# Final norm and first sliding layer's norm joined behind the projection, and squares added in pairs for the mLSTM output norm

## The reference, cut to what matters

```python
def rmsnorm(x, g):
    y = xf * lax.rsqrt(jnp.mean(xf * xf, axis=-1, keepdims=True) + EPS)
    return (y * g.astype(jnp.float32)).astype(x.dtype)

# first_block ends:   x = x + squared_relu_mlp(rmsnorm(x, ff_ln[l]), ff_w1[l], ff_w2[l])
#                     return rmsnorm(x, final_ln)
# second_block:       h = concatenate([meta, x]); for each layer: u = rmsnorm_2(h, norm_gain[i]); h = h + mixer(u)
# mlstm_branch ends:
    h = rmsnorm_2(h, h_gain.reshape(B_HEADS, B_DV)).reshape(bsz, lp, B_W)
    return (h * jax.nn.silu(z.astype(jnp.float32))).astype(u.dtype) @ w_out
```

## Time and profile before

| | before |
|---|---|
| time, median of 3 runs | 3629.98 us (3616.33 to 3632.56) |
| the profiled execution: time | 3631.66 us |
| the profiled execution: span from first to last instruction | 3629.8 us |
| mean granted TensorE clock | 0.976 |
| busy: TensorE matmul | 3461.8 us (95%) |
| busy: TensorE weight load (overlaps the matmuls) | 2727.9 us (75%) |
| busy: VectorE | 1997.6 us (55%) |
| busy: ScalarE | 716.1 us (20%) |
| busy: GpSimd | 84.5 us (2%) |
| moved by DMA | 251.98 MB, mean 69 GB/s |

### The profile page before, as it was taken

How to read it: one execution, slowest core, us unless ns; L and a number is a source line. 1 busy time by engine, 2 the same in 40 slices (tenths; PEclk the granted TensorE clock), 3 DMA queues, 4 the chain that set the end, 5 groups by cost and what they waited for, 6 DMA issues and landing times.

```text
span 3629.8 us, 43978 instructions
## 1 busy us (share of the span) xinstructions
PE 3461.8 (95%) x16715; PEld 2727.9 (75%) x16715; DVE 1997.6 (55%) x4671; ACT 716.1 (20%) x1763; POOL 84.5 (2%) x100
## 2 busy tenths in 40 slices
PE   8987999999999999999999898999999999999988
PEld 3365688888854558888888765888887888887766
DVE  4353167554413783675544658644354656557566
ACT  2221011110012560111100125012212111121143
POOL 0000000000000000000000011000000000000110
PEclk9988999999999999999999999999999999999999
DMA  3100322222211003212222130222211222102311
GB/s 129 49 21 12 111 74 70 82 93 82 105 58 47 13 19 112 80 70 82 93 82 93 59 94 14 92 70 76 73 65 45 95 80 86 43 24 83 110 43 47
DMA packets 39367, 251.98 MB, mean 69 GB/s; under 512 B 5708, under 2 KB 5836, under 8 KB 11008
## 3 DMA queue, kind: packets, MB, share of 16 engines
q1 hardware_dynamic: 31616, 224.41, 17.5%
q10 hardware_dynamic: 4496, 11.89, 1.2%
q0 software_dynamic: 3056, 12.96, 1.1%
HBM read 240.58 MB, written 2.16 MB: 67 GB/s over the span
## 4 chain that ended last, share of the span: by engine, by line
PE 88%; DVE 8%; issue 2%; ACT 1%; DMA 1%; ACTq 0%; POOL 0%; POOLq 0%; DVEq 0%
PE PL L1213 26%; PE PX L1213 20%; PE PL L921 14%; PE PL L1561 4%; PE PL L1408 3%; PE PL L905 2%; PE PX L1670 2%; DVE SCR L2971 2%; PE PL L1326 1%; DVE SCR L2986 1%; PE PL L1586 1%; PE PX L1346 1%; PE PL L1713 1%; PE PX L931 1%; PE PL L1375 1%
## 5 line engine op out<-in xcount | busy, mean ns | idle before, releaser
L921 PE MATMUL PL<-xn,ring 128*128 128x264 f32 (+1 forms) x1600 | 506.6, 474 | 10.8 <-DVE xn L2365 10.2
L921 PEld LDWEIGHTS PL<-xn,ring 128*128 128x128 f32 x1600 | 305.8, 193 | 198.1 <-issue 165.4
L2408 DVE TENSOR_TENSOR Z<-PL,SCR 128x512 f32<-128x512 f32 (+3 forms) x104 | 63.8, 614 | 469.8 <-PE PL L921 372.0
L1213 PE MATMUL PL<-Z,ring 128*128 128x256 f32 (+1 forms) x1248 | 297.3, 388 | 10.5 <-DVE Z L3361 8.6
L1213 PEld LDWEIGHTS PL<-Z,ring 128*128 128x128 f32 x1248 | 240.7, 193 | 49.9 <-DVE Z L3361 10.1
L1213 PE MATMUL PL<-AUX,ring 128*128 128x256 f32 (+1 forms) x1056 | 243.9, 379 | 0.0
L1213 PEld LDWEIGHTS PL<-AUX,ring 128*128 128x128 f32 x1056 | 200.6, 190 | 27.6 <-DVE AUX L2739 0.2
L1213 PE MATMUL PL<-xn,ring 128*128 128x264 f32 (+1 forms) x864 | 204.1, 388 | 12.7 <-DVE xn L2365 11.5
L1213 PEld LDWEIGHTS PL<-xn,ring 128*128 128x128 f32 x864 | 165.7, 192 | 43.1 <-issue 12.4
L1841 ACT ACTIVATE SCR<-PL 128x256 f32<-128x256 f32 (+1 forms) x72 | 27.7, 384 | 737.1 <-PE PL L1213 737.1
L1213 PE MATMUL PX<-Z,AUX 128*128 128x264 f32 (+1 forms) x704 | 163.8, 384 | 2.7 <-DVE Z L3169 2.7
(11 more groups left out here) (515 smaller groups left out, 6055.2 us busy)
## 6 DMA issues: line engine op xcount, KB each, us to landing
ring<-w_tiles SPq DMA_DIRECT2D x212, 1024.0 KB, 4.8
Z<-Z ACTq DMA_DIRECT2D x16, 264.0 KB, 5.1
SCR<-head_rows POOLq DMA_DIRECT2D x16, 264.0 KB, 3.7
AUX<-norm_scratch POOLq DMA_DIRECT2D x8, 528.0 KB, 6.6
cst<-consts ACTq DMA_DIRECT2D x1, 2188.5 KB, 14.9
resid<-x ACTq DMA_DIRECT2D x4, 512.0 KB, 8.8
AUX<-mem POOLq DMA_DIRECT2D x2, 1024.0 KB, 5.1
AUX<-w_cmp POOLq DMA_DIRECT2D x1, 2048.0 KB, 10.6
```

Of the source, the lines that this page charges most:

```text
L921: mm = pe.matmul(PL[:, 2 * h + c, 0:e - a], ring[t % 2][:, k, P * h:P * h + P], src_block(name, k)[:, a:e], start=k == 0, stop=k == KB - 1)
L1213: mm = pe.matmul(ps, lhs(k), rhs(k), start=kc == 0 and k == 0, stop=kc == per - 1 and k == 3)
L2408: ins = dve.tensor_tensor(d, ps, f, ALU.mult)
```

## The change

**The two norms are joined.** With r the final norm's factor of a token, f its gain and g the gain of A0's norm, the input of A0_in is x f g times one factor per token, since r cancels but for epsilon: the factor is 1 / sqrt(mean(x^2 f^2) + eps (mean(x^2) + eps)). `prepare("final", b)` now writes x f g into `X2` inside f21 as each block is finished. Beside the plain sum of squares, VectorE keeps one weighted by f^2 (`joint_squares`, into `joint_acc`), and joins the two after the head sums. `joint_tables`, ahead of the work of f21's tile 9, makes the products of the gains and does the 16 meta columns. TensorE's ones-sum of the joint squares stands behind m7 of A0_in's first tile, its ones-sum of the final norm ahead of the second tile's m1. The final norm is applied to the residual stream in A0_in: its reciprocal after tile 1, its products after tiles 2 and 3, four blocks each. A0 comes ahead of the final norm in the table of norms, and A0's products use PSUM banks as A1's do. POOL's load of a small table for A0 still waits for the final norm to be applied.

**Squares in pairs.** Ahead of the copies of the first three units, VectorE adds the mLSTM's squares two by two in place, and TensorE sums 8 pairs and not 16 blocks: 3, 3 and 2 behind the three units.

```diff
--- before
+++ after
-CONSTS = [("ones", 128), ("eps", 2), ("ident", 128), ("half_swap", 128),
+CONSTS = [("ones", 128), ("eps", 3), ("ident", 128), ("half_swap", 128),
...
+_norm("A0", 0, 1)
 _norm("final", 8, 1)
-_norm("A0", 8, 1)
...
-            if name[:2] == "A0":
-                at = 2
-            elif at is None:
+            if at is None:
...
+        joint_gain, final_squared = tiny[:, 216:224], tiny[:, 224:232]
+        joint_acc = AUX[:, 9792:9792 + T2]
+        meta_sq = AUX[:, 9792 + T2:9792 + T2 + 8 * META].rearrange("p (b t) -> p b t", b=8)
...
+                if name == "A0":
+                    pe.wait_ge(joint_done, 1)
+                    for c, a, e in halves(T):
+                        mm = pe.matmul(PX[:, at + c, 0:e - a], K("ones"), joint_acc[:, a:e], start=True, stop=True)
+                    mm.then_inc(joint_sum, 1)
+                    return
+                if name == "final":
+                    at = 1
+                    pe.wait_ge(norm_std, rooted("A0"))
...
+            def pair_row_sum(p):
+
+                N = NORM["B_h"]
+                at = 2 * (N["index"] % 2)
+                pe.wait_ge(pair_sum, p + 1)
+                for c, a, e in halves(T2):
+                    mm = pe.matmul(PX[0:8, at + c, 0:e - a], K("sum_row", 7 - p, 15 - p),
+                                   sq_buf[:, (N["block0"] + 2 * p) % 4, a:e], start=p == 0, stop=p == 7)
+                mm.then_inc(norm_sq_used, 2)
...
-                                if prepared and prepared[:2] != "xa":
+                                if prepared and prepared[:2] != "xa" and prepared != "A0":
                                     norm(prepared)
                             pe.wait_ge(qd_s, QUAD_TILE0[name] + t + 1)
+                        if name == "A0_in" and (t, i) == (0, 4):
+                            norm("A0")
+                        if name == "A0_in" and (t, i) == (1, 0):
+                            norm("final")
...
-                        for b in range(6 * i, min(6 * i + 6, 16)):
-                            row_sums("B_h", b)
+                        for p in range(3 * i, min(3 * i + 3, 8)):
+                            pair_row_sum(p)
...
-                    act.wait_ge(*((final_block, b + 1) if b < 7 else (norm_done, normed("final"))))
...
-                act.wait_ge(norm_sq_used, N["block0"] + N["per"] * N["groups"])
+                if name == "A0":
+                    act.wait_ge(joint_sum, 1)
+                else:
+                    act.wait_ge(norm_sq_used, N["block0"] + N["per"] * N["groups"])
                 act.wait_ge(norm_done, N["before"]) if N["before"] else None
-                rows = P if N["groups"] == 1 else N["groups"]
-                act.activation(pair(std_buf[0:rows, N["index"] % 2, 0:T], T), psb(PX[0:rows], 2 * (N["index"] % 2), T),
-                               ACT.Sqrt, scale=inv, bias=K("eps", 0, 1)[0:rows]).then_inc(norm_std, 1)
+                rows, eps = P if N["groups"] == 1 else N["groups"], 2 if name == "A0" else 0
+                at = 1 if name == "final" else 2 * (N["index"] % 2)
+                act.activation(pair(std_buf[0:rows, N["index"] % 2, 0:T], T), psb(PX[0:rows], at, T),
+                               ACT.Sqrt, scale=inv, bias=K("eps", eps, eps + 1)[0:rows]).then_inc(norm_std, 1)
...
+                    if i == 0 and g == 1:
+                        norm_root("final")
...
-                if name != "final":
-                    ins = dve.tensor_scalar(dst[b], src[b], gain[b], None, ALU.mult)
+                if name == "final":
+                    ins = dve.tensor_scalar(X2[:, b, META:T2], src[b], joint_gain[:, b:b + 1], None, ALU.mult)
                     ins.then_inc(*((norm_done, 1) if b == 7 else (xn_block, 1)))
+                    if 2 <= b < 7:
+                        joint_squares(b - 1)
+                        add_squares(name, b - 1)
+                    return
+                ins = dve.tensor_scalar(dst[b], src[b], gain[b], None, ALU.mult)
+                ins.then_inc(*((norm_done, 1) if b == 7 else (xn_block, 1)))
                 if b >= 2:
                     add_squares(name, b - 1)
                 if b == 7:
                     add_squares(name, 7)
+
+            def joint_squares(b):
+
+                first, tokens = NORM["final"]["block0"], joint_acc[:, META:T2]
+                if b == 1:
+                    dve.wait_ge(norm_sq, first + 1)
+                    counted(dve.tensor_scalar(tokens, acc_buf[:, 0:T1], final_squared[:, 0:1], None, ALU.mult))
+                dve.wait_ge(norm_sq, first + b + 1)
+                dve.wait_ge(dve_step, own[0])
+                counted(dve.scalar_tensor_tensor(tokens, sq_buf[:, (first + b) % 4, 0:T1], final_squared[:, b:b + 1], tokens,
+                                                 ALU.mult, ALU.add))
+
+            def joint_tables():
+
+                final, first = Q("final_ln"), Q("norm_gain", 0, 8)
+                counted(dve.tensor_tensor(joint_gain, final, first, ALU.mult))
+                counted(dve.tensor_tensor(final_squared, final, final, ALU.mult))
+                meta = resid[:, :, 0:META]
+                for b in range(8):
+                    dve.tensor_scalar(X2[:, b, 0:META], meta[:, b, :], first[:, b:b + 1], None, ALU.mult)
+                step(dve.tensor_tensor(meta_sq, meta, meta, ALU.mult))
+                step(dve.tensor_tensor(meta_sq[:, 0:4], meta_sq[:, 0:4], meta_sq[:, 4:8], ALU.add))
+                step(dve.tensor_tensor(meta_sq[:, 0:2], meta_sq[:, 0:2], meta_sq[:, 2:4], ALU.add))
+                counted(dve.scalar_tensor_tensor(joint_acc[:, 0:META], meta_sq[:, 0, :], D * (EPS - EPS * EPS) / P,
+                                                 meta_sq[:, 1, :], ALU.add, ALU.add))
...
-                        if name == "final" and b:
-                            ins.then_inc(final_block, 1)
...
+                    if name == "f21" and t == 9:
+                        joint_tables()
...
-                    for b in range(8):
-                        dve.wait_ge(*((final_block, b + 1) if b < 7 else (norm_done, normed("final"))))
-                        prepare(n, b)
                     dve.wait_ge(norm_done, normed(n))
                     sums_head(n + "_in", 0, (0, 4))
+                    for b in (6, 7):
+                        joint_squares(b)
+                        add_squares("final", b)
+                    dve.wait_ge(norm_sq_used, NORM["final"]["block0"] + 7)
+                    dve.wait_ge(dve_step, own[0])
+                    tokens = joint_acc[:, META:T2]
+                    dve.scalar_tensor_tensor(tokens, acc_buf[:, 0:T1], EPS, tokens, ALU.mult, ALU.add).then_inc(joint_done, 1)
                     sums_tail(n + "_in", 0, (0, 4))
 
                 def tables(t):
+
+                    if i == 0 and t == 1:
+                        norm("final")
+                    if i == 0 and t in (2, 3):
+                        x, _, gain, _, T = norm_spec("final")
+                        for b in range(4 * t - 8, 4 * t - 4):
+                            ins = dve.scalar_tensor_tensor(x[b], x[b], gain[b], factors("final"), ALU.mult, ALU.mult)
+                        if t == 3:
+                            ins.then_inc(norm_done, 1)
...
+                    for p in range(3 * i, min(3 * i + 3, 8)) if i < 3 else ():
+                        one, two_ = (sq_buf[:, (N["block0"] + 2 * p + j) % 4, :] for j in range(2))
+                        dve.wait_ge(norm_sq, N["block0"] + 2 * p + 2)
+                        dve.tensor_tensor(one, one, two_, ALU.add).then_inc(pair_sum, 1)
...
-    c["eps"] = np.broadcast_to(np.array([EPS, 1.0])[None, :], (P, 2))
+    c["eps"] = np.broadcast_to(np.array([EPS, 1.0, EPS * EPS])[None, :], (P, 3))
```

More of the change, by code:

```diff
@@ L251, in build @@
         out_sem = sem("out_sem")
-        final_block = sem("final_block")
+        pair_sum = sem("pair_sum")
+        joint_done, joint_sum = sem("joint_done"), sem("joint_sum")
         dn_kk, dn_d, dn_exp, dn_at = (sem(n) for n in ("dn_kk", "dn_d", "dn_exp", "dn_at"))
@@ L462, in build @@
         assert 2 * (NORM["xa1"]["index"] % 2) == 0 and 2 * (NORM["ff1"]["index"] % 2) == 2
-        assert [2 * (NORM[n]["index"] % 2) for n in ("A0", "B", "C", "A1")] == [2, 0, 0, 0]
+        assert [2 * (NORM[n]["index"] % 2) for n in ("A0", "B", "C", "A1")] == [0, 0, 0, 0]
         xk, xv = blocks(Z, MEM, 16, 8), blocks(Z, MEM, 24, 8)
@@ L1750, in _ @@
                     nsa()
-                elif layer == "final":
-                    norm("final")
                 elif layer in ("win0", "win1"):
@@ L1756, in _ @@
                     mlstm()
-                else:
+                elif layer == "hgrn":
                     hgrn()
@@ L1793, in prepared_square @@
                         act.wait_ge(x_in[0], 16)
-                    elif host is None:
-                        act.wait_ge(psum_free, evacuated("f21"))
                     else:
@@ L2324, in _ @@
```

(4 more changed lines are left out.)

5 lines of the change are left out of this document (2 added, 3 removed).

## The result

| | this kernel | before | ratio | 95% interval |
|---|---|---|---|---|
| median of 11 runs each, us | 3610.98 (3603.65 to 3612.53) | 3628.36 (3616.33 to 3632.56) | 0.9948 | 0.9941 to 0.9956 |
| profiled execution, us (span; granted clock) | 3603.65 (3601.9; 0.980) | 3631.66 (3629.8; 0.976) | | |

The ratio makes it 18.9 us or 0.52% faster (0.44 to 0.59% by the interval). That is just beyond the 0.5% which the prediction took for the least that can be told from no change, and the interval reaches to both sides of it. The forecast was 3608. The two profiled executions lie 28.0 us apart and not 18.9, since that of after is the shortest of its runs.

A forecast was written before the change was run, and what follows sets the result against it. TensorE was taken to bound the kernel (busy 95% of the span, 88% of the chain). Savings of 17.6 + 4.6 = 22.2 us take the profiled 3631.66 to 3609.5; with the median 1.7 lower, forecast 3608, range 3598 to 3622.

The forecast's parts named there:

- Part one: From f21's last matmul to tile 1 of A0_in: joining the norms saves 17.6 us.
- the wait at m6: In A0_in's first tile, TensorE waits 1.3 us at product m6 for VectorE's two head sums.
- the tail sum that m5 needs: In A0_in's first tile, VectorE's tail sum is ready within 0.2 us of when m5 needs it.
- The split of it: Of the saving before A0_in's tile 1, some 12.5 us is idle time and 5.1 the half clock.
- The moved work: VectorE's work moved into f21 and A0_in is covered by its idle time and costs nothing.
- Rival C: VectorE's moved work in A0_in is not hidden and costs 8.7 us: 13.5 gained, 3616 us; chance 0.08.
- Part two: Row sums in B_z: pairs save 4.6 us, 7.3 without waits, with two new TensorE waits of 1.3 us.
- Rival B: In B_z ScalarE's squares pace the sums, so pairs save towards nothing: 17.6 us alone, 3612; chance 0.10.
- D: No wait at m6 of A0_in and none in B_z's row sums: 26.2 us gained, 3604; chance 0.07.
- Rival A: Three short TensorE pauses of about 1.3 us also lower the clock, 5.1 us per fall: 3613 to 3618; chance 0.12.
- Rival E: Slower: the clock stays low in A0_in after the pause is gone; all at half gives +53 us, 3683; chance 0.03.
- The sum, 22.2: Whole kernel: 17.6 us before A0_in's tile 1 plus 4.6 us in B_z make 22.2 us saved.

The follow-up runs named there:

- experiment 9: The kernel before with eighteen needless matmuls behind the final norm's ones-sum, so that TensorE keeps working; one execution, 3626.23 us.
- experiment 7: The changed kernel with the final norm's reciprocal and all eight products in one piece after tile 1 of A0_in; one execution, 3602.87 us.
- also alone: The kernel before with only the mLSTM's squares summed in pairs, without the joined norms; ratio 0.9991 to the kernel before.
- experiment 8: The changed kernel with the joint ones-sum behind m2 of A0_in's first tile and not behind m7; one execution, 3617.16 us.
- the three comparisons: The changed kernel, unedited, run three times against the kernel before; ratios 0.9948, 0.9943 and 0.9944.

## Why the prediction was right, and where its steps were off

The forecast of 3608 with "faster" as the likeliest held: 3610.98. Point by point:

**Part one, minus 17.6.** Measured minus 17.97; tile 1 stands at 15.28 or 15.29 in all seven traces that have this order. The order of events was as worked: block 7 in time for the eighth matmul, m6 waiting for the head sums, the joint sum free of waiting, tile 1 at 15.28 and not 15.7. The term mis-sized is the wait at m6: the step was "TensorE waits 1.3 us", and it is 1.00 from start to start (0.84 as a gap). VectorE came through sooner than durations set one after another gave, because rows overlap by their tails: from the scaling of block 6 to the end of that of block 7 it took 2.72 us, and I had 2.9. Another 0.2 was put down for the tail sum that m5 needs; TensorE had no wait there (m5, m3 and m4 take 5.34 us from 1996.27 to 2001.61).

**The split of it was wrong.** "Some 12.5 of this is idle time and 5.1 the half clock" takes m1 and m2 from 7.9 us busy to 3.6 as if TensorE alone paced them. The row of the second head sum shows that VectorE would have held m6 back anyway, and in experiment 9 four of m1's records at full clock gained nothing. By the rows the half clock had on the path the final ones-sum (0.85) and at most 0.45 at m6; the rest of the 18 us is VectorE's chain. The sum was right since I compared both ends of the stretch, not because I knew what lay in between.

**The moved work.** Costed at nothing, and nothing is what it cost: TensorE has no wait behind any of it. joint_tables took 2.16 us where I took 2.5, and TensorE waits nowhere in the tiles around it. But the reason given, "each piece is shorter than the 4.24 us that VectorE idles between a tile's end and the next m2", is not the limit (and the idle time ends with m6, not m2): experiment 7 put 8.7 us into one piece and TensorE did not wait. So "nothing" was right for a reason that was wrong. Rival C falls.

**Part two, minus 4.6.** Measured minus 4.56, also alone. The waits were put at 1.3 and are 1.12 each, and 4.05 us for a group of three pairs, which I had at 4.0. Rival B falls, since ScalarE's pace does not reach the other six pairs, and D falls, since the waits are there.

**Rival A** falls for this change: the clock is 1.00 behind the pauses of 0.84 and 1.12 us. The Trainium skill ("TensorE: Matmul & The Clock Gate", section "A second HAM failure mode: psum-queue depth-cycling") tells of a kernel in which TensorE idles briefly between groups of matmuls so often that the clock swings between its two levels. These pauses, one or two at a time between long work, showed none of that. The one of 4.09 us in experiment 8 and the 2.30 us of the earlier trace rows did go with a fall. Nor can the rival be set aside by the length of a pause, as the prediction did with "no row here shows a fall behind a pause of 1.3 us": in experiment 9 the clock fell in a wait of 1.33 us, shortly behind one of 1.00. **Rival E** falls: A0_in had 1.00 throughout. The half clock of the earlier trace rows lies in a run of 32 records of one column each (from 1050.41 to 1055.73), and A0_in has nothing like it.

**The sum, 22.2.** The touched stretches give 22.5, the three comparisons 18.9, 20.7 and 20.3. Of the 1.8 to 3.6 us between them 0.8 has a place, which the prediction did not name: "to B_z" is 0.7 to 0.9 us longer in seven of the eight traces with the joined norms (1.5 in that of experiment 8). There the clock falls sooner. TensorE, behind a wait for ScalarE's small copy, takes 2.12 us for four short records, and 1.33 in the kernel before: after the change the clock is down during the wait (0.53 from 2092 to 2093), and before it falls only as these records end (0.95 from 2116 to 2117, 0.50 from 2117 to 2118). After, then before:

```profile
2094.11 2.12 PE L1473 MATMUL PX<-SCR,AUX 20*128 20x264 f32 x4 [3.32 <-ACT tiny L2144]
```

```profile
2116.06 1.33 PE L1447 MATMUL PX<-SCR,AUX 20*128 20x264 f32 x4 [3.29 <-ACT tiny L2118]
```

Why, with nearly the same wait, is open; there was no run on it. What is left, 1 to 3 us, also stays open, and the traces do not hold it. The three traces of the changed kernel span 3601.9, 3606.1 and 3607.5 us against 3629.8 and 3630.1 for the two of the kernel before, which is 22 to 28 us less and not 19 to 21. In part that is so because both traces of the kernel before lie above the median of their runs, by 3.3 and 1.5 us. The untouched stages go with their low-clock time and swing by more than what is left (f21's end by 4.2 us over the three traces of the changed kernel, by 11 over all). So it is either chance of the runs or a loss of clock in executions that were not traced, and these runs can't say which.

## What to carry to other kernels

Cost a stretch from its two ends, and before naming what fills it ask of each slow piece whether the next one had its inputs sooner: a half clock beside a chain on another engine that takes as long costs next to nothing. Work moved onto an engine with slack may be covered for longer than its idle gap: ask when its next result is due (experiment 7). And where untouched stages swing by more than the change, take the distances of the touched ones from each trace, run the control, and do not believe one comparison of five runs.
